# Expert rows gathered by pair instead of by token, and summed by VectorE and TensorE together

## The reference

```
out[t] = sum over the 128 pairs p of  gate[t, p] * gelu(x[t] . u[e(t, p)]) * v[e(t, p)]
```

## Time and profile before

| what | us |
|---|---|
| time, median of 3 runs | 2264.06 (2261.77 to 2265.73) |
| span of the profiled execution, first to last instruction | 2353.7 |
| TensorE busy | 2044.5 |
| VectorE busy | 1177.2 |
| GpSimd busy | 1001.2 |
| ScalarE busy | 650.0 |

### The profile page before, as it was taken

One profiled execution on the slowest core, in us unless ns is written; L12 is line 12 of the kernel. 1 busy time (PEld: TensorE's weight loads), 2 busy tenths in 40 slices (PEclk: granted clock), 3 DMA queues, 4 the chain that ended last, 5 costly groups with the idle time before them and its releaser, 6 DMA issues.

```text
span 2353.7 us, 38380 instructions
## 1 busy us (share of the span) xinstructions
PE 2044.5 (87%) x14289; PEld 1496.2 (64%) x14289; DVE 1177.2 (50%) x3447; ACT 650.0 (28%) x977; POOL 1001.2 (43%) x874
## 2 busy tenths in 40 slices
PE   9889999999997667889898889999999986777777
PEld 4554899999995323334356346999999973233332
DVE  2554699423333533578456834997233333333333
ACT  1332244545551001112134022454555520000000
POOL 0111469830004565656514303688500026666665
PEclk9899999999998798999997989999999998888878
DMA  6473434444447999999932334244444469999998
GB/s 233 173 279 119 144 129 159 161 162 162 168 163 264 331 355 369 362 329 335 350 122 62 90 116 152 81 161 153 162 168 164 165 217 348 360 346 357 365 357 312
DMA packets 179914, 529.91 MB, mean 225 GB/s; under 512 B 22066, under 2 KB 49234, under 8 KB 179474
## 3 DMA queue, kind: packets, MB, share of 16 engines
q0 software_dynamic: 87296, 310.68, 36.3%
q1 hardware_dynamic: 91282, 216.25, 26.8%
q10 hardware_dynamic: 1152, 0.52, 0.1%
HBM read 524.69 MB, written 2.69 MB: 224 GB/s over the span
## 4 chain that ended last, share of the span: by engine, by line
PE 68%; another core or an unknown queue 8%; DVE 8%; POOL 5%; issue 5%; DMA 3%; ACT 2%; SPq 1%; DVEq 0%; ACTq 0%; PEldq 0%
PE bank L950 10%; PE bank L952 10%; PE bank L951 10%; PE bank L769 8%; PE bank L1014 8%; PE bank L990 4%; POOL u_low L703 3%; PE bank L1032 3%; PE bank L1092 2%; DVE i_one_hot L2172 2%; DMA v_slot<-in_peer_v,v_rows 2%; POOL v_slot L712 2%; PE bank L979 1%; PE bank L1242 1%
## 5 line engine op out<-in xcount | busy, mean ns | idle before, releaser
L712 POOL DMA_INDIRECT v_slot<-in_peer_v,v_rows x417 | 394.6, 946 | 703.8 <-PE bank L952 441.1
L950 PE MATMUL bank<-h_parts,u_high 128*128 128x288 f32 x2048 | 607.0, 296 | 7.9 <-POOL u_low L703 6.2
L951 PE MATMUL bank<-h_parts,u_high 128*128 128x288 f32 x2048 | 604.4, 295 | 0.0
L952 PE MATMUL bank<-h_parts,u_low 128*128 128x288 f32 x2048 | 602.8, 294 | 0.0
L950 PEld LDWEIGHTS bank<-h_parts,u_high 128*128 128x128 f32 x2048 | 384.1, 188 | 11.6 <-POOL u_low L703 9.6
L952 PEld LDWEIGHTS bank<-h_parts,u_low 128*128 128x128 f32 x2048 | 385.8, 188 | 0.0
L951 PEld LDWEIGHTS bank<-h_parts,u_high 128*128 128x128 f32 x2048 | 384.6, 188 | 0.0
L1597 ACT CAST u_high<-u_slot 128x1024 fp32r<-128x1024 f32 x256 | 268.7, 1050 | 400.5 <-PE bank L952 249.1
L703 POOL TENSOR_TENSOR u_low<-u_slot,u_high 128x1024 fp32r<-128x1024 f32 x120 | 321.1, 2686 | 93.5 <-ACT u_high L1597 93.4
L1014 PE MATMUL bank<-v_slot,weight_columns 128*32 128x512 f32 x1412 | 274.1, 687 | 57.3 <-DMA v_slot<-in_peer_v,v_rows 34.1
L1014 PE MATMUL bank<-v_slot_of_columns,weight_columns 128*32 128x512 f32 x636 | 246.2, 687 | 69.8 <-DVE weight_columns L2179 44.0
(11 more groups left out here) (393 smaller groups left out, 2463.2 us busy)
## 6 DMA issues: line engine op xcount, KB each, us to landing
u_slot<-in_peer_ut SPq DMA_DIRECT2D x256, 512.0 KB, 3.5
w_q<-in_peer_w_q SPq DMA_DIRECT2D x8, 2048.0 KB, 14.4
region<-in_cache_a_kt SPq DMA_DIRECT2D x8, 960.0 KB, 11.8
region<-in_cache_a_v SPq DMA_DIRECT2D x8, 960.0 KB, 11.4
v_slot<-in_peer_v,v_rows POOLq DMA_INDIRECT x417
region<-in_ev_w_in SPq DMA_DIRECT2D x3, 2048.0 KB, 15.1
region<-in_pool_kv POOLq DMA_DIRECT2D x40, 128.0 KB, 5.0
ckv_t_norm<-in_pool_ckv SPq DMA_DIRECT2D x64, 64.0 KB
```

Of the source, the lines that this page charges most:

```text
L712: pool.indirect_dma_start(out=VS[l][slot], out_offset=None, in_=v_rows, in_offset=bass.IndirectOffsetOnAxis(ap=IDX[:, at:at + 1], axis=0)) ...
L950: pe.matmul(bank, uh, HR[:, 0, c, :], start=(c == 0), stop=False)
L951: pe.matmul(bank, uh, HR[:, 1, c, :], start=False, stop=False)
L952: ins = pe.matmul(bank, ul, HR[:, 0, c, :], start=False, stop=(c == KC - 1))
```

## The change

A gather now fetches, for one pair k, the rows of all 128 tokens of a tile: a slot holds pair k with tokens on partitions (for the samples, 32 gathers of four copies of 32 tokens, a copy for each two heads). The number of gathers (288 a layer) and the bytes stay. The weight of a row is then a scalar for each partition, and the sum over pairs needs no sum over partitions:

- VectorE does `ACC_DVE = row * weight + ACC_DVE` on 128x1024, the accumulator in two banks of PSUM. Each waits for the one before.
- For some pairs of the prompt tiles (`by_tensor`: 37 of tile 0 in both layers, 45 of tile 1 in layer 0, 60 in layer 1) TensorE multiplies by a diagonal matrix of the weights, which ScalarE makes (`DIAG`), and sums in two more banks. VectorE is left with 91 of tile 0, and 83 or 68 of tile 1; it has all 32 of the samples.

All tokens of a tile must be picked before its first value is used: picked values go to `HP`, are transposed by TensorE (`turn_weights`) and multiplied by the gates. VectorE's list becomes: 8 sample groups; 32 groups of tile 0 with one sample value each; 32 groups of tile 1 with four pairs of tile 0 each; then tile 1's pairs, and beside these, in layer 0, the S5 work, the key norms and the odd norm. The samples' four copies are summed by a matmul (`sum_samples`). ScalarE makes the one-hot in two passes (absolute difference, then 1 minus it, cut at 0); the spread is one matmul of 512 columns in place of four of 128. `turn_route` transposes the second index only and makes the new layout of the first by four matmuls. Gathers also wait for the landing of the gather eight before. Slots are planned anew: layer 0 has 9 + 19, of which 14 end with tile 0, layer 1 has 9 + 20. The weight columns, their zeroing and the five clearing matmuls fall away.

```diff
-GROUPS = [("sample", q) for q in range(NS // 4)] + [(t, j) for t in range(2) for j in range(32)]
+GROUPS = [(2, j) for j in range(NS // 4)] + [(t, j) for t in range(2) for j in range(P // 4)]
...
+GATHERS = [(2, k) for k in range(NS)] + [(t, k) for t in range(2) for k in range(P)]
...
+LANDINGS = 8
...
+def by_tensor(l, t, k):
+
+    if t == 2 or k >= P - 8:
+        return False
+    if t == 0:
+        return k % 16 in (2, 5, 8, 11, 14)
+    return k % 2 == 1 if l else k % 8 in (2, 5, 7)
...
+        V_COLUMNS = ([(picked_at(7), HB[k] + 8192, "picked_full", 8, PROMPT0_LAST) for k in (0, 2)]
+                     + [(picked_at(15 + 8 * m), HB[k] + D * m, "picked_full", 16 + 8 * m, PROMPT0_LAST) for m in range(4) for k in range(4 if m >= 2 else 2)]
+                     + [(picked_at(47 + 8 * m), HB[k] + 4096 + D * m, "picked_full", 48 + 8 * m, len(GATHERS)) for m, k in ((0, 1), (1, 1), (2, 1), (3, 1), (3, 0))],
+                     [(picked_at(7), HB[k] + 8192, "picked_full", 8, len(GATHERS)) for k in range(4)]
+                     + [(picked_at(15 + 8 * m), HB[k] + D * m, "picked_full", 16 + 8 * m, len(GATHERS)) for m in range(4) for k in range(4)])
...
                     pool.wait_ge(sem(signal), before_layer[signal] + count)
-                    at = hidden_column(t)
+                    if landed > 16:
+
+                        pool.wait_ge(sem(name), landed - 16)
+                    at = P * t + k
                     pool.indirect_dma_start(out=VS[l][slot], out_offset=None, in_=v_rows,
-                                            in_offset=bass.IndirectOffsetOnAxis(ap=IDX[:, at:at + 1], axis=0)).then_inc(sem(f"v_loaded{slot}"), 16)
+                                            in_offset=bass.IndirectOffsetOnAxis(ap=IDX[:, at:at + 1], axis=0)).then_inc(sem(name), 16)
...
+                    for i in range(4):
+                        out = bank[group_rows(t), i * P:i * P + P]
                         if t < 2:
-                            ins = pe.transpose(bank[:, j * P:j * P + P], ROUTE[:, t, j, :], ident)
+                            ins = pe.matmul(out, ident[:, i:P:4], ROUTE[:, t, 0, :], start=True, stop=True)
...
+                    pe.matmul(banks[q % 2][:, :], ident16[R, R.start + j:R.start + j + 1].broadcast_to([R.stop - R.start, P]),
+                              I1G[R].rearrange("p i k -> p (i k)"), start=True, stop=True).then_inc(sem("i1_spread"), 1)
...
+                        pe.wait_ge(sem("diagonal_ready"), n)
+                        name, landed = landing(l, g)
+                        pe.wait_ge(sem(name), landed)
                         for h in range(2):
-                            for i in range(4):
-                                ins = pe.matmul(banks[6 - 2 * kind + h][32 * i:32 * i + 32, :], WZ[:, 4 * (q % 4) + i, 31 - j:63 - j],
-                                                slots[i][:, 512 * h:512 * h + 512], start=False, stop=False, skip_group_check=True)
-                    ins.then_inc(sem("v_used"), 1)
+                            ins = pe.matmul(banks[6 + h][:, :], DIAG[:, n % 4, :], VS[l][slot][:, 512 * h:512 * h + 512], start=first, stop=(TURN[l][g] == PE_UP_TO[l][t]),
+                                            skip_group_check=True)
+                        ins.then_inc(sem("v_used_by_pe"), 1)
...
+                link(act.activation(flat, banks[q % 2][:, :], ACT.Abs, bias=NPCOL))
+                act.activation(flat, flat, ACT.Relu, bias=ONE, scale=-1.0).then_inc(sem("one_hot_ready"), 1)
...
+                        act.activation(DIAG[:, n % 4, :], ident, ACT.Copy, scale=WT[:, P * t + k:P * t + k + 1]).then_inc(sem("diagonal_ready"), 1)
...
+                    for i, t in enumerate(group_tokens(GROUPS[q])):
+                        picked = banks[2 + q % 2][:, i * P:i * P + P]
+                        ins = dve.scalar_tensor_tensor(out=picked, in0=iota, scalar=I2T[:, t:t + 1], in1=picked, op0=ALU.is_equal, op1=ALU.mult,
+                                                       accum_out=HP[:, t:t + 1])
+                    ins.then_inc(sem("pairs_picked"), 1)
...
+                        if k == 0:
+
+                            dve.wait_ge(sem("weights_ready"), 3 * l + (t + 1) % 3 + 1)
+                        else:
+                            dve.wait_ge(sem("v_used_by_dve"), n - 1)
+                        name, landed = landing(l, g)
+                        dve.wait_ge(sem(name), landed)
+                        if k == 0:
+                            ins = dve.tensor_scalar(ACC_DVE[:, :], VS[l][slot], w, None, ALU.mult)
+                        else:
+                            ins = dve.scalar_tensor_tensor(out=ACC_DVE[:, :], in0=VS[l][slot], scalar=w, in1=ACC_DVE[:, :], op0=ALU.mult, op1=ALU.add)
+                        ins.then_inc(sem("v_used_by_dve"), 1)
...
+                    if q == LAST_OF[2] + 1:
+                        token_weights(2)
+                    if LAST_OF[2] < q <= LAST_OF[0]:
+                        values(2, [q - LAST_OF[2] - 1])
+                    if q == LAST_OF[0]:
+                        add_samples_of_rows()
+                    if q == LAST_OF[0] + 1:
+                        token_weights(0)
+                    if q == LAST_OF[0] + 2:
+                        add_sample()
+                    if q == NGR - 1:
+                        add_pe_sums(0)
+                        token_weights(1)
+                    if q > LAST_OF[0]:
+                        values(0, range(4 * (q - LAST_OF[0] - 1), 4 * (q - LAST_OF[0])))
```

More of the change, by code:

```diff
@@ new lines, in by_tensor @@
+def by_tensor(l, t, k):
[4 more added lines that the diff above has]
+    return k % 2 == 1 if l else k % 8 in (2, 5, 7)
+TURN = [[n + 1 for n in range(0)] for _ in range(2)]
+for l_ in range(2):
+    counts_ = [0, 0]
+    for t_, k_ in GATHERS:
+        counts_[by_tensor(l_, t_, k_)] += 1
+        TURN[l_].append(counts_[by_tensor(l_, t_, k_)])
+USED_BY_DVE = [sum(not by_tensor(l_, *g_) for g_ in GATHERS) for l_ in range(2)]
+USED_BY_PE = [sum(by_tensor(l_, *g_) for g_ in GATHERS) for l_ in range(2)]
@@ L295, in build @@
+        V_PLAN = []
+        for l_, columns in enumerate(V_COLUMNS):
             places = V_FIRST + columns
-            V_PLAN.append(value_plan([(when, slot, signal, count, last) for slot, (when, _, signal, count, last) in enumerate(places)], landings))
-        VS = [[tile_at(f"v_slot{n}" if n < NVS else f"v_slot_of_columns{l}{n}", [D], at) for n, (_, at, *_) in enumerate(V_FIRST + V_COLUMNS[l])]
+            V_PLAN.append(value_plan(l_, [(when, slot, signal, count, last) for slot, (when, _, signal, count, last) in enumerate(places)]))
@@ new lines, in sum_samples, with values @@
+                def sum_samples():
+                    pe.wait_ge(sem("samples_added"), l + 1)
+                    for h in range(2):
+                        ins = pe.matmul(banks[7][32 * h:32 * h + 32, :], SUMM, X[:, 2, 512 * h:512 * h + 512], start=True, stop=True)
+                    ins.then_inc(sem("samples_summed"), 1)
+                def values(t, j):
+                    for k in range(4 * j, 4 * j + 4):
+                        if not by_tensor(l, t, k):
+                            continue
+                        g = GATHERS.index((t, k))
+                        slot = V_PLAN[l][g][0]
+                        n = l * USED_BY_PE[0] + TURN[l][g]
+                        first = n == l * USED_BY_PE[0] + (1 if t == 0 else PE_UP_TO[l][0] + 1)
+                        if first and t == 0:
+                            pe.wait_ge(sem("x_tile_updated"), 6 * l + 4)
+                        elif first:
+                            pe.wait_ge(sem("pe_sums_added"), 2 * l + 1)
+                        pe.wait_ge(sem("diagonal_ready"), n)
+                        name, landed = landing(l, g)
+                        pe.wait_ge(sem(name), landed)
@@ L1826, in _ @@
                 peer(1)
+                picks(1)
+                for j in range(1, P // 4):
+                    diagonals(1, 1, j)
         @block.vector
@@ new lines, in used, with add_samples_of_rows, add_sample @@
+                def used(t):
+                    dve.wait_ge(sem("v_used_by_dve"), l * USED_BY_DVE[0] + TURN[l][GATHERS.index((t, NS - 1 if t == 2 else P - 1))])
+                def add_samples_of_rows():
+                    used(2)
+                    dve.tensor_tensor(X[:, 2, :], X[:, 2, :], ACC_DVE[:, :], ALU.add).then_inc(sem("samples_added"), 1)
+                def add_sample():
+                    dve.wait_ge(sem("samples_summed"), l + 1)
+                    for h in range(2):
+                        x = X[0:NS, 2, 512 * h:512 * h + 512]
+                        TT(x, x, banks[7][32 * h:32 * h + 32, :], ALU.add)
+                    say("x_tile_updated")
@@ L2208, in peer @@
+                add_tile(0)
+                for j in range(P // 4):
+                    values(1, range(4 * j, 4 * j + 4))
+                    if j == P // 4 - 2:
+                        add_pe_sums(1)
```

(7 more changed lines are left out.)

391 lines of the change are left out of this document (210 added, 181 removed).

## The result

| what | before | after |
|---|---|---|
| time, median, us | 2264.2 | 2331.09 (2329.61 to 2335.72) |
| ratio | | 1.0291, 95% interval 1.0273 to 1.0309 |
| span of the profiled execution, us | 2353.7 | 2333.2 |

The change makes the kernel 67 us slower. The forecast was +5 us, so it has the sign and misses the size, and the measured time lies outside the range of 2246 to 2292. The two spans seem to say the reverse of the times, 2333.2 after against 2353.7 before. That riddle is the centre of this case.

The account below looks back on a forecast made before the run. Gather transfers were taken to bound the value stages, TensorE the hidden ones. Layer 0's stage +5 (passing to VectorE), layer 1's -3 and turning the routes +3 gave +5 us on 2264.06: 2269 us, range 2246 to 2292.

Parts of the forecast that it names:

- that surplus: The profiled span's 89.6 us above the median, placed in the hidden stages, so the value stages' 5 us carried over unscaled.
- 369 GB/s for a full queue: Gather transfers in the value stages: 1.42 us for each gather, 409 us for a layer's 288.
- A value 1.31 us: Each VectorE row-times-weight addition on 128x1024 takes 1.31 us, with 1.23 and 1.37 as the ends.
- Rival B: A VectorE value takes only 1.23 us, its scalar fetched under the operation before: 2250 us; chance 0.27.
- P 99 us: Each value stage's first part, picks up to the weights of tile 0, with the sample values on VectorE: 99 us.
- The price of the order: Transfers starve during tile 0's picks: 12 to 18 gathers, some 17 to 26 us a layer, idle.
- Tile 0 159 us: Tile 0's values beside tile 1's picks take 159 us, set narrowly by VectorE, with transfers at 155.
- Tile 1 of layer 0 206 us: Layer 0's last part is bound by VectorE's values plus its other work: 206 us, the stage ending at 464.
- Tile 1 of layer 1: Layer 1's last part is bound by transfers at 1.42 us a gather: stage 431 us against 434, -3.
- Rival C: TensorE falls to its lower clock level in the picks: 2287 us, chance 0.20; deep form through tile 0 about 2390, 0.03.
- Rival D: Gather descriptors on GpSimd starve beside VectorE's long values, one gather each 1.87 us: 2455 us; chance 0.03.
- Rival E: Transfers bind the value stages as before and nothing is seen, within 0.2%: 2264 us; chance 0.05.

Follow-up runs that it names:

- e5: The kernel before, unchanged, profiled again on the chip of the second comparison: 2266.44 us.
- e11: The changed kernel with TensorE taking 60 instead of 45 of layer 0's tile 1 pairs, VectorE 68 instead of 83: 2317.56 us.
- e12: The changed kernel with 32 needless VectorE maxima over 128x1024 added to each layer's tile 1, one after every four pairs: 2376.71 us.
- e8: The changed kernel with TensorE's diagonal products made for the first 512 columns only, except the first and last of each tile: 2326.6 us.
- e7: The changed kernel with the samples' values summed over the first 64 of 1024 columns only, gathers and slots kept: 2301.85 us.
- e6: The changed kernel, unchanged, run on the same chip as e5: 2331.49 us, ratio 1.0294.
- e15: The changed kernel with each gather waiting for the landing four before instead of eight before: 2448.49 us, ratio 1.0809.
- e1: The kernel before, unchanged, profiled again on the chip of the first comparison: 2357.66 us.
- e2: The edit of e11 to the changed kernel, run on the same chip as e1: 2418.92 us, ratio 1.0265.

## Why the prediction was wrong

**The step that failed** is the last: "The hidden stages [...] are the likeliest place of that surplus; the value stages hang on transfers and long operations, so I carry the 5 us over one to one". The 89.6 us sat in the value stages (e5 against rows 2: 44.6 + 46.0). The baseline for both stages was thus too long, 459 and 434 us where the timed kernel has 414.5 and 388.2, and so was "I take 369 GB/s for a full queue": that is a rate with the stops in it. In e5 and after, full slices show about 409 GB/s, a gather in 1.28 us. The two stages before were 91 us too long in the sum and the two after 29 us (895 against 866); the difference is the 62 us of the miss.

The same sum with these two numbers: layer 0, bound by VectorE, stays at 464, so 464 - 414.5 = +49.5. Layer 1 is 99 + 231 x 1.28 + 4 = 399, so +11. With +3 that is +63, 2327 us against 2331 measured. A stage that is bound by an engine doesn't shrink with its transfers. That is why the error didn't cancel in layer 0, and why the size was missed by a factor of over ten while the lengths after were nearly right. That it comes within 4 us is partly luck: by it layer 0's stage is 5 us too long (464 against 459) and layer 1's 8 us too short (399 against 407). The trace held two warnings. The span stood 89.6 us above the median, and VectorE's idle time in rows 7 was ended for 34.8 and 55.7 us by "remote", in a program that runs on one core.

**The steps one by one.**

- *Bytes and bounds.* Right in kind: layer 0 passes from the transfers to VectorE (e11, e12), layer 1 stays with the transfers (e12, +3.8 us for 39 us of VectorE's work; e8, no change of its 403 us for half of TensorE's products).
- *A value 1.31 us.* Right. It takes 1.29 us, and three in a row take 3.94, 1.31 each. Rival B, 1.23 us, falls. So does the PSUM charge that the prediction took from the Trainium skill (VectorE: DVE Perf Modes, "The TRN2 errata"): with both operands in SBUF the 128x1024 operation takes 1222 ns, with one in a bank 1218.

In order of time on VectorE, tile 1 of layer 0 after:

```profile
1103.48 3.94 DVE L2300 SCALAR_TENSOR_TENSOR banks<-v_slot,token_weights,banks 128x1024 f32<-128x1024 f32 x3
```

- *P 99 us.* 91 to 95. The 32 groups take (816.8 - 742.7) / 32 = 2.32 us, not 2.53: the 0.15 us for waits and some of the value's hand-off aren't there, while the part ahead of the first sample value takes 17 and 21 us, not 15. ScalarE's two passes are 687 and 722 ns where I took about 600 each; it works 59 of P's 91 us, so this cost nothing. What e7 was expected to show, ScalarE as the next bound of P, its trace doesn't: TensorE is the nearer one, busy 64.9 of 69.7 us, and 16.1 of VectorE's 16.9 us of idle time end with its picks, while ScalarE works 59.1.
- *The price of the order*, 17 to 26 us a layer. The count of gathers was right: GpSimd has started 54 and 60 by the end of P (forecast 55 and 61), where the kernel before has started 63 and 73 in 94 us (e5). These 9 and 13 gathers are 12 and 17 us at 1.28 us, and layer 1's stage, which transfers bind on both sides, is 14.6 us longer in e6 than in e5. e7 takes 24 and 20 us out of P, and the stages fall by 14.5 and 11.3 us. So the order has a price of about 11 to 17 us a layer, less than forecast.
- *Tile 0 159 us.* 155 to 157. VectorE sets it narrowly, as written (e8 rules out TensorE, and VectorE doesn't wait for gathers there).
- *Tile 1 of layer 0 206 us.* 211.
- *Tile 1 of layer 1.* The form was right; the 1.42 us was wrong.
- *Turning the routes +3 us.* The hidden stages come to +2.9 and -4.1 us in e6, -1.2 in sum. The -4.1 wasn't followed up.
- *The wait for the eighth gather before, nothing.* At eight the stretches run at 408 GB/s, so it holds, but by about 1 us: four in flight cost 120 us (e15).
- *Rival C.* TensorE's clock is 0.81 and 0.82 in P, between its two levels, and 0.89 in tile 0. It doesn't become the bound: P is VectorE's (e7), and tile 0 isn't TensorE's (e8). *Rival D* falls: gathers take 962 and 951 ns in layer 0 beside the long values. Before, they took 951 and 971. The rule of the Trainium skill that the prediction weighed (SBUF - State Buffer, "SBUF: two separate sides") agrees with that: a value has only one of its two inputs in SBUF.
- *Rival E* falls with the ratio.

**Beyond the two kernels.** e11 is the fastest complete variant and still 51 us above before (ratio 1.0227). Taking away the samples' values altogether would give 30 us more at most by e7, 22 us short even if both add up. No version seen here beats the kernel before, which already runs layer 1's stage in 388 us, where 288 gathers at 1.28 us are 369.

## What to carry to other kernels

Before a difference is worked out, the traced execution has to be the one that was timed: where span and median disagree by 4%, look for idle time that nothing in the program ends, compare the whole idle time of each group with that of an execution without it, and price every term once with it and once without. A change that trades a transfer bound for an engine bound costs more the faster the transfers really are. And making an operand usable only when a whole tile is ready has a price in slots: here 9 at the start, and 11 to 17 us of transfer time in each stage.

## What the runs showed of the hardware

- The same program takes 2266 us on three chips and 2358 us on a fourth. The difference is in the stages with gathers only (e1 against e5). GpSimd stops for 2.2 us once in eight gathers, every 11.8 us, and its idle time ahead of the gathers of layer 1's stage is 161.7 us in e1 where it is 104.1 in e5. In the changed kernel on that chip the stops are of about 3 us, 10 to 16 gathers apart (e2). The cause is open.
- Gathers of 128 rows of 4 KB saturate at 409 GB/s. GpSimd issues one each 1.24 us (0.94 us busy, 0.30 between), which is hardly less than the 1.28 us that the transfer of one takes. GpSimd itself would be the next bound of these stages.
- Issue to landing is 14.3 us in the kernel before, which has no limit but its slots (e5, 2030 to 2150 us), 8.3 with eight in flight and 5.7 with four, and only the last costs bandwidth: 409, 408 and 324 GB/s.
- Two ScalarE passes over 128x512 took 687 (out of a bank) and 722 ns (within SBUF), both with a bias for each partition, where the squaring of the same size out of a bank takes 596 ns.
